# Fewer candidate sums in a top-16 choice, gate sets from an earlier tile, a third slot for a streamed matrix, and expert weights asked for one phase later

## The reference

```python
v1, i1 = top_k(s1, 16)                     # s1, s2: [512 tokens, 8 heads, 128 keys]
v2, i2 = top_k(s2, 16)
cand = (v1[..., :, None] + v2[..., None, :]).reshape(t, 8, 256)
sc, ci = top_k(cand, 16)
idx = i1[ci // 16] * 128 + i2[ci % 16]
gates = softmax(sc)
out = sum(gates * gelu(h @ peer_u[idx]) * peer_v[idx])   # per token, over heads and the 16
...
aff = softmax(h @ w_router); gate, idx = top_k(aff.T, 64)    # 16 experts, 64 tokens each
y = (silu(xs @ w_gate) * (xs @ w_up)) @ w_down               # per expert, added to its tokens
```

## Time and profile before

| | us |
|---|---|
| median of three runs | 3162.68 |
| the profiled execution | 3163.25 |
| its span, from the first to the last instruction | 3161.4 |
| TensorE matmul busy | 2672.5 |
| VectorE busy | 1345.5 |
| ScalarE busy | 834.9 |
| GpSimd busy | 974.4 |
| bytes moved | 869.99 MB |

### The profile page before, as it was taken

The page is one execution under the profiler, slowest core; times in us unless marked ns, Lnnn a source line. Parts: engine busy times, 40 slices in busy tenths (PEclk is TensorE's granted clock), DMA queues, the critical chain, the costliest instruction groups (busy, mean ns, idle before and its releaser), DMA issues. The chain is left out here.

```text
span 3161.4 us, 34451 instructions
## 1 busy us (share of the span) xinstructions
PE 2672.5 (85%) x12721; PEld 1850.8 (59%) x12721; DVE 1345.5 (43%) x2317; ACT 834.9 (26%) x1407; POOL 974.4 (31%) x485
## 2 busy tenths in 40 slices
PE   5986687999999995999999599964988788888886
PEld 2853577999999995877778476652323223222222
DVE  4346534995877765565665524444000000000001
ACT  2224221333666662333333222331000000000001
POOL 0030001666777775878878202000000000000000
PEclk8977788999999998999999799987999999999999
DMA  5333132445899998999999323117999999999996
GB/s 219 119 135 110 67 107 62 164 164 188 267 344 364 347 343 318 342 341 338 331 338 341 125 87 109 53 57 310 422 421 421 421 421 422 421 421 421 421 422 281
DMA packets 271859, 869.99 MB, mean 275 GB/s; under 512 B 28927, under 2 KB 122751, under 8 KB 219128
## 3 DMA queue, kind: packets, MB, share of 16 engines
q1 hardware_dynamic: 215136, 703.71, 58.7%
q0 software_dynamic: 38016, 138.43, 11.6%
q10 hardware_dynamic: 18584, 26.23, 2.2%
HBM read 812.69 MB, written 55.60 MB: 275 GB/s over the span
## 5 line engine op out<-in xcount | busy, mean ns | idle before, releaser
L562 PE MATMUL dots_dot_ps<-one_acts,dots_u_split 128*128 128x384 f32 x3072 | 556.5, 338 | 22.8 <-POOL dots_u_split L87 22.4
L689 PE MATMUL val_banks<-val_v,val_coef_split 128*128 128x512 f32 x2304 | 531.6, 391 | 43.5 <-DVE val_coef_split L87 43.0
L562 PEld LDWEIGHTS dots_dot_ps<-one_acts,dots_u_split 128*128 128x128 f32 x3072 | 534.0, 189 | 30.9 <-issue 22.6
L689 PEld LDWEIGHTS val_banks<-val_v,val_coef_split 128*128 128x128 f32 x2304 | 430.6, 188 | 144.3 <-issue 55.8
L934 PE MATMUL moe_up_ps<-all_raw_first,all_h_rows 128*64 128x512 f32 x1696 | 419.7, 605 | 69.3 <-DMA all_raw_first<-in_w_up 49.6
L87 POOL TENSOR_TENSOR dots_u_split<-dots_u_raw,dots_u_split 128x1024 fp32r<-128x1024 f32 x128 | 332.0, 2595 | 417.0 <-ACT dots_u_split L82 416.0
L934 PEld LDWEIGHTS moe_up_ps<-all_raw_first,all_h_rows 128*64 128x64 f32 x1696 | 138.8, 138 | 317.8 <-issue 316.6
L87 POOL TENSOR_TENSOR val_v<-val_v_raw,val_v 128x2048 fp32r<-128x2048 f32 x64 | 297.5, 4649 | 82.3 <-ACT val_v L82 82.2
L1053 DVE TENSOR_TENSOR all_x<-moe_y_ps,all_x 128x512 f32<-128x512 f32 x64 | 44.0, 691 | 560.6 <-PE moe_y_ps L900 560.5
L653 DVE SCALAR_TENSOR_TENSOR val_banks<-val_v_rows,one_slot_coef,val_banks 128x1024 f32<-128x1024 f32 x128 | 164.2, 1283 | 208.2 <-DMA val_v_rows<-in_peer_v,one_expert 208.0
L951 PE MATMUL moe_y_ps<-all_raw_first,moe_hid_t 128*64 128x512 f32 x848 | 206.8, 605 | 41.9 <-DMA all_raw_first<-in_w_down 22.8
(11 more groups left out here) (354 smaller groups left out, 3216.6 us busy)
## 6 DMA issues: line engine op xcount, KB each, us to landing
all_raw_first<-in_w_gate SPq DMA_DIRECT2D x106, 1024.0 KB, 27.3
all_raw_first<-in_w_up SPq DMA_DIRECT2D x106, 1024.0 KB, 27.6
all_raw_first<-in_w_down SPq DMA_DIRECT2D x106, 1024.0 KB, 27.3
dots_u_raw<-in_u_tiles SPq DMA_DIRECT2D x128, 512.0 KB, 4.4
val_v_raw<-in_peer_v SPq DMA_DIRECT2D x64, 1024.0 KB, 5.0
expert_dots<-dots_gelu ACTq DMA_DIRECT2D x128, 192.0 KB, 4.8
expert_weights<-pe_shared SPq DMA_DIRECT2D x48, 512.0 KB, 8.1
val_dot<-expert_dots SPq DMA_DIRECT2D x64, 384.0 KB
```

Of the source, the lines that this page charges most:

```text
L562: last = self.nc.tensor.matmul(self.banks[:, j, 0:DENSE], self.split[:, j, u_part, k], self.h_t[:, h_part, k, T - DENSE:T], start=(k == 0 ...
L689: last = nc.tensor.matmul(banks[:, 2 * (t + 1) + half, :], coef_split[:, b, c_part, a, t * P:(t + 1) * P], v[:, b, v_part, a, half * BANK: ...
```

## The change

- **Candidates.** Of the 16 by 16 sums per head only the first 4 rows in full and the first 4 columns of the other 12 rows are formed: 4*16 + 12*4 = 112. `best16` works on 112 elements in place of 256. The place in the shorter list is turned back into row and column by six more instructions of 128 elements per token tile.
- **Gate sets.** `FIRST` is 50 in place of 56, `LEFT` 78 in place of 72. `after_tile` is 4 + 68n//48 in place of 4 + 4n//3. The 128 gathers are spread over 78 tiles.
- **Third slot.** `ExpertDots` has three raw and three split slots. The third raw slot is the first block's buffer `h_row` (one row tile of 128 tokens), which VectorE copies to PSUM at the phase's start; SP therefore waits for that copy ahead of its first load. The third split slot is the part of `h_t` that belongs to the first 128 tokens, with a row pitch of 512 elements. The PSUM banks and gelu buffers stay at two (`OUT`). The load of tile n now waits for the low part of tile n-3, the high part of tile n for the dot of tile n-3. The order of instructions on each engine is the same. The hardware loops hold 6 tiles in place of 2.
- **Expert weights.** Pieces 6 to 13 are asked for at the start of the expert phase, with pieces 14 to 16, and no longer at the end of the router phase.

```diff
 class ExpertDots:
-    SLOTS = 2
+    SLOTS, OUT = 3, 2
...
-    def load(self, sp, tile, turn, j):
+    def load(self, sp, tile, loop, q):
         sp.wait_ge(self.lo_ready, tile + 1)
...
+        self.raw = [raw[:, i] for i in range(n - 1)] + [h_row[:].rearrange("p (k e) -> p k e", k=KD)]
+        self.split = [split[:, i] for i in range(n - 1)] + [h_t[:, :, :, 0:P]]
...
 class ExpertPieces:
-    FIRST, MORE = 14, 3
+    FIRST, MORE, EARLY = 14, 3, 6
...
-                for n in range(pieces.FIRST, pieces.ring):
+                for n in range(pieces.EARLY, pieces.ring):
                     pieces.load(sp, n)
...
-    CHOICE, LAG, SET = 28, 4, 8
+    FIRST, LAG, SET = 50, 4, 8
+    HEAD, BACK = 4, 4
+    CAND = HEAD * PK + (PK - HEAD) * BACK
...
-        after_tile = [LAG + 4 * n // 3 for n in range(SETS)]
+        after_tile = [LAG + (LEFT - 10) * n // SETS for n in range(SETS)]
...
-                with sp.Fori(0, CHOICE) as i:
-                    for j in range(2):
-                        dots.load(sp, i * 2 + j, i, j)
+                sp.wait_ge(h_ready, 1)
+                with sp.Fori(0, LOOPS) as i:
+                    for j in range(LOOP):
+                        dots.load(sp, i * LOOP + j, i, j)
...
-                with act.Fori(0, CHOICE - 1) as i:
-                    for j in range(2):
-                        dots.split_scalar(act, i * 2 + (j + 2), i + 1, j)
-                        dots.activate(act, i * 2 + j, i, j)
+                with act.Fori(0, LOOPS) as i:
+                    for j in range(LOOP):
+                        dots.split_scalar(act, i * LOOP + (j + 2), i, j + 2)
+                        dots.activate(act, i * LOOP + j, i, j)
...
-                    step(nc.vector.tensor_tensor(
-                        cand, val[:, 0::2, :].unsqueeze(3).to_broadcast([P, PH, PK, PK]),
-                        val[:, 1::2, :].unsqueeze(2).to_broadcast([P, PH, PK, PK]), ALU.add))
+                    for i0, rows_, columns, c0 in ((0, HEAD, PK, 0), (HEAD, PK - HEAD, BACK, HEAD * PK)):
+                        step(nc.vector.tensor_tensor(
+                            cand[:, :, c0:c0 + rows_ * columns].rearrange("p h (i j) -> p h i j", i=rows_),
+                            val[:, 0::2, i0:i0 + rows_].unsqueeze(3).to_broadcast([P, PH, rows_, columns]),
+                            val[:, 1::2, 0:columns].unsqueeze(2).to_broadcast([P, PH, rows_, columns]), ALU.add))
...
+                    step(nc.vector.tensor_copy(place_f, place[:].rearrange("p h k -> p (h k)")))
+                    step(nc.vector.tensor_scalar(over, place_f, float(-HEAD * PK), 0.0, ALU.add, ALU.max))
+                    step(nc.vector.scalar_tensor_tensor(out=over, in0=over, scalar=float(PK // BACK - 1), in1=place_f,
+                                                        op0=ALU.mult, op1=ALU.add))
+                    step(nc.vector.tensor_copy(place[:].rearrange("p h k -> p (h k)"), over))
+                    step(nc.vector.tensor_scalar(back, place_f, float(HEAD * PK), float(BACK) / PK - 1.0, ALU.is_ge,
+                                                 ALU.mult))
...
+                        if i == 1:
+                            step(nc.vector.scalar_tensor_tensor(out=to, in0=back, scalar=1.0, in1=to, op0=ALU.add,
+                                                                op1=ALU.mult))
...
 def logits_phase(nc, A, ident, x, h_row, h_dram, rows_stored, logit_t, rstd, pieces):
-    EARLY = 6
...
                     sp.dma_start(h_dram[t * P:(t + 1) * P, :], h_row[:, t, :]).then_inc(rows_stored, 16)
-                for n in range(EARLY, pieces.FIRST):
-                    pieces.load(sp, n)
```

More of the change, by code:

```diff
@@ L561, in dot @@
             for i, (u_part, h_part) in enumerate(((0, 0), (0, 1), (1, 0))):
-                last = self.nc.tensor.matmul(self.banks[:, j, 0:DENSE], self.split[:, j, u_part, k],
+                last = self.nc.tensor.matmul(self.banks[:, q % 2, 0:DENSE], self.split[q % 3][:, u_part, k],
                                              self.h_t[:, h_part, k, T - DENSE:T],
@@ L1141, in peer_first_phase @@
     with Scope(nc, "peer") as s:
-        cand = shared[:, at:at + PH * PK * PK].rearrange("p (h i j) -> p h i j", h=PH, i=PK)
-        at += PH * PK * PK
+        cand = shared[:, at:at + PH * CAND].rearrange("p (h c) -> p h c", h=PH)
+        at += PH * CAND
+        place_f, over, row_f, column_f, back = (shared[:, at + i * P:at + (i + 1) * P] for i in range(5))
+        at += 5 * P
         hot = shared[:, at:at + PH * PK * PK].rearrange("p (s i) -> p s i", i=PK)
@@ L1191, in _ @@
                 sp.dma_start(iota[:], rows(A["iota"], P)).then_inc(iota_loaded, 16)
-                with sp.Fori(0, CHOICE) as i:
-                    for j in range(2):
-                        dots.load(sp, i * 2 + j, i, j)
+                sp.wait_ge(h_ready, 1)
+                with sp.Fori(0, LOOPS) as i:
+                    for j in range(LOOP):
+                        dots.load(sp, i * LOOP + j, i, j)
+                for j in range(FIRST - LOOPS * LOOP):
+                    dots.load(sp, LOOPS * LOOP + j, LOOPS, j)
                 def store_part(span, part):
@@ L1203, in _ @@
                 for r in range(LEFT):
-                    dots.load(sp, FIRST + r, (FIRST + r) // 2, r % 2)
+                    dots.load(sp, FIRST + r, (FIRST + r) // LOOP, (FIRST + r) % LOOP)
                     while part < PARTS * SPANS and r >= after_tile[PER_SPAN * (part // PARTS + 1) - 1] + 4 + part % PARTS:
@@ L1217, in _ @@
                 dots.credits(pool, "gpsimd")
-                with pool.Fori(0, CHOICE - 1) as i:
-                    for j in range(2):
-                        dots.split_pool(pool, i * 2 + j, i, j)
-                for r in range(-2, LEFT):
-                    dots.split_pool(pool, FIRST + r, (FIRST + r) // 2, r % 2)
+                with pool.Fori(0, LOOPS) as i:
+                    for j in range(LOOP):
+                        dots.split_pool(pool, i * LOOP + j, i, j)
+                for r in range(LOOPS * LOOP - FIRST, LEFT):
+                    dots.split_pool(pool, FIRST + r, (FIRST + r) // LOOP, (FIRST + r) % LOOP)
                     if r == -1:
@@ L1233, in _ @@
                 dots.credits(pe, "tensor")
-                with pe.Fori(0, CHOICE) as i:
-                    for j in range(2):
-                        dots.dot(pe, i * 2 + j, i, j)
-                for r in range(LEFT):
-                    dots.dot(pe, FIRST + r, (FIRST + r) // 2, r % 2)
+                with pe.Fori(0, LOOPS) as i:
+                    for j in range(LOOP):
+                        dots.dot(pe, i * LOOP + j, i, j)
+                for r in range(LOOPS * LOOP - FIRST, LEFT):
+                    dots.dot(pe, FIRST + r, (FIRST + r) // LOOP, (FIRST + r) % LOOP)
                     if r == 1:
@@ L2170, in _ @@
                 sp.dma_start(g_rows[:], rows(A["norm2_g_2"][0], P)).then_inc(g_loaded, 16)
-                for n in range(EARLY):
+                for n in range(pieces.EARLY):
                     pieces.load(sp, n)
```

70 lines of the change are left out of this document (36 added, 34 removed).

## The result

The changed kernel takes **3137.8 us** (median of 6 runs, 3133.1 to 3141.6) where the kernel before, beside it, takes 3161.5 (3154.8 to 3169.3): ratio **0.9924, 95% interval 0.9909 to 0.9939**. It is faster, by more than 0.3%, and inside the range of 3112 to 3142. But of the forecast's 39.0 us only 24.8 came in the profiled execution (3138.45, span 3136.6). The table gives the differences by stages. The choice starts at 528.79 before and at 528.65 after, so the lengths can be compared.

What follows compares the result with a forecast made beforehand. It took TensorE to bound the first PEER phase and the expert-weight stream the end; -11.6 - 7 - 14.0 - 1 + 0.6 + 3 - 4 - 5 = -39.0 us gave 3124, range 3112 to 3142.

Steps and rivals of the forecast that it cites:

- (a): Dots during the choice: with a third slot a low part of 3.87 us has two dots' time; 11.6 us less.
- Fewer candidates: VectorE's choice: shorter scans and sums, less six added instructions at 7.0 us, make it 23 us shorter; none counts by itself.
- Sets from tile 50: Start of the gate sets: VectorE has the choice at 733, 12 us ahead of tile 49's dot end at 745.
- R4: Rival: the choice is late after all, each us past 745 costing one; 3135 with none off; chance 0.02.
- (b): Last dots before the first set: the four gathers no longer hold TensorE; 7 us of 7.8 go.
- (c): Places with two dots between sets: ScalarE's high part is done earlier, 1.48 us lost becomes 0.43; 14.0 us less.
- (e): Start of the first PEER phase: SP's first load waits for VectorE's copy to PSUM; 0.6 us more.
- (f): Six spans of sets: next u load queues behind SP's wait for the last set, delaying ScalarE; 3 us more.
- The tail: Last dot's end to last gathered row's dot: last gathers are issued a dot earlier; 4 us less.
- R2: Rival: TensorE's larger loop body pays a whole load's landing at each of 7 jumps back; 3155; chance 0.05.
- R3: Rival: GpSimd's low part in the third split slot, rows 512 elements apart, is dear; 3176 at 7.2 us; chance 0.02.
- R1: Rival: sets miss their gain, two-dot places still costing 1.0 to 1.48 us or (f) at its upper bound; 3139; chance 0.17.

Runs made afterwards that it cites:

- the last experiment: The kernel before (two slots, 256 candidates, sets from 56) with the choice's places and indices as numbers moved to idle PSUM banks: 3160.2 us, ratio 0.9970.
- the PSUM kernel: The changed kernel with the choice's small tensors (places, row, column, indices as numbers) moved from SBUF to idle PSUM banks: 3125.3 us, ratio 0.9880 against the kernel before.

## Why the prediction was right or wrong

By its own steps, in the profiled executions.

- **The third slot, (a)**: 11.6 us, right in size. Right in cause as far as it went (low parts of 3.87 us don't fit into one dot's time), but the last experiment shows that they are long because VectorE holds them (2.42 us on average without it, for 2.86), and that the slot is one of two cures.
- **Fewer candidates: the step that failed**, "Six added instructions of 128 elements at 0.29 [...] cost 7.0. In all 23 us off." The scans gave their 25 us (L1329, 0.261 for 0.416). In place of the rest: the added instructions cost 14, the sums lost 2 and not 4.9, the third slot itself lengthens the choice by 8, and other instructions on SBUF were held more often. The choice grew by 1.7.
- **Sets from tile 50**, "VectorE has it at 733, 12 us ahead": it had it at 757.9, 12 us late. This is R4, which was given 0.02: with nothing off the choice it forecast 3135. Its measured 3138 is that and 3 us more. R4's chance was set by the sum of bare durations, though the prediction itself says of the low parts that they reach 3.87 us "only with VectorE at the same memory": it saw GpSimd held by VectorE and did not ask what that does to VectorE.
- **(b), the hand-over**: 7 us forecast to go, but 11.4 are lost now where 7.8 were, so 10.6 of the missing 14.2 us. 4.5 of the 11.4 are the lower clock behind two waits, and before, too, a part was ("10.0 us in place of 8.3"), which the prediction saw and did not name. "The four gathers at r = -1 no longer hold TensorE" failed as well: they do, for 2.05 us here and 3.51 in the kernel without index arithmetic. In the changed kernel the later wait for the choice covers that.
- **(c), the two-dot places**: 1.48 became 0.48 to 0.49, for a forecast of 0.43. The stretch from the first set to the last dot lost 14.7 us, 13 forecast, 25.0 before.
- **(e)** 0.6 as forecast: the first high part starts 2.2 us after the choice's start, for 1.6 before. **(f)** came only at the last span, as ScalarE's waits of 5.52, 4.11 and 2.60 us for u tiles from 1164 on, of which 2.4 reached TensorE; 3 forecast.
- **The tail**: 5.0 for 4. **Expert weights**: 4.2 in the changed kernel, 6 in the other traces, for 5. The first expert matmul comes 52.0 us after the router's first one, for 56.4; behind it 337 GB/s flow for 8 us where 147 did, and from it to the end it is 959.4 us for 959.1. In the middle the time is 1.9 longer, within what unchanged code varies.
- **A larger loop**: no price seen. The casts stay 4.16 us apart over the 8 turns of six tiles. R2 and R3 did not happen: the low parts of the third slot take 2.66 us on average during the choice, those of the others 2.84.

The sum closes: 10.6 (hand-over) + 1.7 (sets) + 1.9 (middle) + 0.8 (expert weights) - 1.0 (tail) = 14.0, for 14.2 missing. That the range held was luck in part: it reached to 3142 for R1, whose mechanism did not happen, and R4's loss fell into it.

## What to carry to other kernels

An instruction's price on VectorE beside a busy GpSimd is not its bare duration: look at the minimum and the maximum of each form, not at the mean, and count how many short instructions on SBUF stand in the critical chain; each may cost a whole instruction of the other engine, or two in a row. The gathers that GpSimd issues are held in the same way. Before taking work off such a chain, move an operand of it into PSUM that lies idle: here it took 28 us off the choice and 12.5 us off the changed kernel, for no work. And ask first whether the chain is waited for. To the last dot the third slot alone, with sets from 56, is as far (643.2 us) as the PSUM kernel with the short list and sets from 50 (642.8): PSUM gave back what the earlier start had lost. Of the four parts of the change the third slot and the expert weights carry the gain. The shorter list gave none in any kernel here, and the earlier start none but perhaps 4 us of the tail; the slot and the weights alone were not run together.

## What had not been expected of the hardware

- A cast of 128 elements takes 0.23 us, and 2.42 when it starts 0.06 us into a GpSimd subtraction on SBUF of 2.40. Integer shifts, subtractions and products of two tensors behave the same; MAX8, FIND_INDEX8, MATCH_REPLACE8 and TENSOR_REDUCE run beside it unchanged. The Trainium skill (VectorE: DVE Perf Modes, section Why PSUM operands drop a tier) says that an operand in PSUM rules out the mode that uses both SBUF ports. With an operand in PSUM the casts of the choice take 0.30 us and are never held. That the mode is the reason no run shows; they show the durations.
- A GpSimd gather is issued in 0.94 us, and in 2.02 to 2.97 beside a VectorE product with both inputs in SBUF; beside one with an input in PSUM it stays at 0.94.
- The granted clock fell to 0.50 behind TensorE's waits of 2.05 and 1.75 us, and the two dots there took 6.02 and 7.15 us for 4.3. That is 4.5 us beside 3.8 of those waits, which a sum of waits leaves out. Behind a wait of 2.67 us in another kernel it did not fall; what decides stays open here.
- The same instructions from the slot gelu to the router took 930.7 to 941.0 us in 14 executions of kernels that differ elsewhere. What sets it stays open. A part of under 5 us is better read in its stretch of the trace than in the medians.
